# A hybrid FoX / HGRN2 / S5 layer on one core: the S5 chunk input with its four lags stacked on the contraction rows, and its weights relaid through DRAM

## What is computed

```python
x = x + 0.5 * swiglu(rms_norm(x, ffn1_norm[l]), ...)
p = rms_norm(x, mix_norm[l]) @ w_in[l]        # split into FoX q,k,v,f; HGRN2 q,f,i,g; S5 u
o_a = fox_attention(q, k, v, a_f + fox_f_bias[l])
o_b = hgrn2(b_q, b_f, b_i, lb) ... * silu(b_g)
o_c = s5_block(c_u, ...)
x = x + concat(o_a, o_b, o_c) @ w_out[l]
x = x + 0.5 * swiglu(rms_norm(x, ffn2_norm[l]), ...)
```

```python
bu = einsum('blgh,gph->blgp', u, bbar)         # real and imaginary part
x_t = lbar * x_{t-1} + bu_t                    # complex, per group and state
y_t = Re(C x_t) + D u_t ; z = gelu(y) ; out = z * sigmoid(z @ glu_w + glu_b)
```

## Time and profile before

| | us |
|---|---|
| median of three runs | 1020.2 (1020.04 to 1020.46) |
| time of the profiled execution | 1020.22 |
| span of the profiled execution | 1018.4 |
| PE busy in it | 1008.6 (99%) |
| DVE busy | 735.3 (72%) |
| ACT busy | 558.9 (55%) |
| POOL busy | 225.7 (22%) |

### The profile page before, as it was taken

The page is one execution under the profiler, slowest core; times in us unless marked ns, Lnnn a source line. Parts: engine busy times, 40 slices in busy tenths (PEclk is TensorE's granted clock), DMA queues, the critical chain, the costliest instruction groups (busy, mean ns, idle before and its releaser), DMA issues.

```text
span 1018.4 us, 20402 instructions
## 1 busy us (share of the span) xinstructions
PE 1008.6 (99%) x8434; PEld 941.2 (92%) x8434; DVE 735.3 (72%) x936; ACT 558.9 (55%) x699; POOL 225.7 (22%) x293
## 2 busy tenths in 40 slices
PE   9999999999999999999999999999999999999998
PEld 8998989999899999999999898999999998989898
DVE  7677787889878666565667867777988767565654
ACT  5646444556587645454476554456466865444441
POOL 0005999600002000000020079994000020000000
PEclk9999999999999999999999999999999999999999
DMA  8745554434325464545455454544442255454541
GB/s 305 271 161 179 192 200 170 167 125 167 111 99 207 166 218 153 213 157 213 182 199 210 158 213 166 205 166 164 138 155 90 107 221 190 184 203 167 199 172 42
DMA packets 26817, 178.38 MB, mean 175 GB/s; under 512 B 3120, under 2 KB 4160, under 8 KB 5760
## 3 DMA queue, kind: packets, MB, share of 16 engines
q1 hardware_dynamic: 25632, 173.03, 46.5%
q10 hardware_dynamic: 1008, 4.05, 1.1%
q0 software_dynamic: 112, 0.40, 0.1%
HBM read 176.42 MB, written 1.05 MB: 174 GB/s over the span
## 4 chain that ended last, share of the span: by engine, by line
PE 89%; DVE 8%; ACT 1%; DMA 1%; issue 1%; SPq 0%; DVEq 0%; ACTq 0%
PE ps L897 24%; PE ps L845 16%; PE ps L846 16%; PE ps L847 16%; PE ps L899 12%; DVE in_lo L1467 1%; DVE lo L1251 1%; DMA raw<-stream 1%; ACT hi L599 1%; PE ps L1007 1%; DVE fqk L1658 1%; PE ps L1056 0%; DVE sc L1674 0%; PE ps L1078 0%; DVE queries L1532 0%
## 5 line engine op out<-in xcount | busy, mean ns | idle before, releaser
L897 PE MATMUL ps<-xg,hi 128*128 128x512 f32 x1120 | 397.8, 399 | 0.3
L1251 DVE TENSOR_TENSOR lo<-raw,hi 128x2048 fp32r<-128x2048 f32 x130 | 303.3, 2359 | 130.8 <-ACT hi L599 130.8
L899 PE MATMUL ps<-xg,lo 128*128 128x256 f32 x1120 | 314.5, 281 | 0.0
L599 ACT ACTIVATE hi<-raw 128x2048 fp32r<-128x2048 f32 x130 | 244.7, 1911 | 108.7 <-PE ps L899 81.8
L897 PEld LDWEIGHTS ps<-xg,hi 128*128 128x128 f32 x1120 | 210.6, 188 | 52.0 <-DVE lo L1251 0.9
L899 PEld LDWEIGHTS ps<-xg,lo 128*128 128x128 f32 x1120 | 211.7, 189 | 0.0
L845 PE MATMUL ps<-act_hi,hi 128*128 128x256 f32 x704 | 199.4, 283 | 0.6 <-DVE act_lo L1304 0.6
L846 PE MATMUL ps<-act_lo,hi 128*128 128x256 f32 x704 | 199.2, 283 | 0.0
L847 PE MATMUL ps<-act_hi,lo 128*128 128x256 f32 x704 | 199.1, 283 | 0.0
L845 PEld LDWEIGHTS ps<-act_hi,hi 128*128 128x128 f32 x704 | 134.8, 191 | 2.9 <-DVE lo L1251 0.8
L847 PEld LDWEIGHTS ps<-act_hi,lo 128*128 128x128 f32 x704 | 135.0, 192 | 0.0
(11 more groups left out here) (325 smaller groups left out, 1695.0 us busy)
## 6 DMA issues: line engine op xcount, KB each, us to landing
raw<-stream SPq DMA_DIRECT2D x160, 1024.0 KB, 4.9
par<-params ACTq DMA_DIRECT2D x2, 1463.0 KB, 8.5
raw<-stream SPq DMA_DIRECT2D x8, 256.0 KB, 7.2
rows<-stream SPq DMA_DIRECT2D x2, 1024.0 KB, 7.0
x<-xT ACTq DMA_DIRECT2D x4, 256.0 KB, 6.8
out<-x SPq DMA_DIRECT2D x8, 128.0 KB, 2.0
con<-consts POOLq DMA_DIRECT2D x1, 373.5 KB, 6.2
mask<-masks POOLq DMA_DIRECT2D x1, 20.0 KB, 7.0
```

Of the source, the lines that this page charges most:

```text
L599: e.activation(hi[slot][:, :], raw[slot][:, :], ACT.Copy).then_inc(hi_written, 1)
L897: pe.matmul(bank(b), hi[slot][:, w:w + P], xg[:, k, :, :].rearrange("p s t -> p (s t)"), start=k == 0, stop=False, skip_group_check=True)
L899: last = pe.matmul(bank(b)[:, 0:T], lo[slot][:, w:w + P], xg_hi[:, k, :], start=False, stop=k == KT - 1, skip_group_check=True)
L1251: v.tensor_tensor(lo[slot][:, :], raw[slot][:, :], hi[slot][:, :].bitcast(F32), ALU.subtract).then_inc(lo_written, 1)
```

## The change

New buffers `ws` (the stacked weights: 128 rows = 4 lags x 32 channels, for both parts and eight state tiles) and `us` (the stacked u) are laid over buffers that are free at that time (`ws` over `fqk`, `us` over `fsq`). POOL writes `w_lag` to a DRAM scratch, and SP reads it back into the rows of `ws`, with the fourth lag read directly from the parameters. ACT and DVE copy u into `us`, half each. `s5_input` becomes 16 products of 128 rows, and it is called two k tiles later. The clear of `fqk` moves behind `bu_done`.

```diff
+        with ExitStack() as early:
+            ws = sb("ws", [P, 2, S5_TILES, P], F32, early)
+            sb("over_fv", [P, 2, 256], F32, early)
+            us = sb("us", [P, S5_TILES, NC], F32, early)
...
+        lag_rows = nc.dram_tensor("lag_rows", (LAG - 1, 2, P, 2 * P), F32, kind="Internal").ap()
+
+        def stack_inputs(op, q):
+
+            for i in range(LAG):
+                last = op(us[32 * i:32 * i + 32, 2 * q:2 * q + 2, :], u[32 * q:32 * q + 32, :, i * NC:(i + 1) * NC])
+            return last
...
# SP
                 for w in range(IN_UNITS):
+                    if w == RING:
+                        sp.wait_ge(units_done, l * SPLIT_UNITS + FFN_UNITS + RING)
+                        sp.wait_ge(lags_stored, l * 16 + 16)
+                        for lag in range(LAG - 1):
+                            sp.dma_start(ws[32 * lag:32 * lag + 32, :, :, :].rearrange("c a (q h) n -> c a q (h n)", h=2),
+                                         lag_rows[lag].rearrange("a (q c) n -> c a q n", c=32)).then_inc(ws_loaded, 16)
+                        for part, name in enumerate(("b_re", "b_im")):
+                            at, size = COLS[name]
+                            sp.dma_start(ws[32 * LAG - 32:, part, :, :].rearrange("c (q h) n -> c q (h n)", h=2),
+                                         params[l][:, at:at + size].rearrange("(q c) n -> c q n", c=32)
+                                         ).then_inc(ws_loaded, 16)
...
# POOL
                 steps.close()
+                pool.wait_ge(tables_ready, l * 2 + 2)
+                pool.dma_start(lag_rows.rearrange("i a r n -> r i a n"), w_lag[:, :, :, :]).then_inc(lags_stored, 16)
 
                 sum_squares(l * 3 + 1)
+                pool.memset(attn[:, :, :], 0.0).then_inc(attn_cleared, 1)
+                pool.wait_ge(bu_done, l + 1)
                 pool.memset(fqk[0:64, :, 1:FOX_HEADS:2, :], 0.0).then_inc(heads_cleared, 1)
-                pool.memset(attn[:, :, :], 0.0).then_inc(attn_cleared, 1)
...
# ACT, between split_in of unit 2 and of unit 3
                 split_in(4)
+                e.wait_ge(proj_dve, l * 9 + 1)
+                for q in (0, 1):
+                    stack_inputs(lambda dst, src: e.activation(dst, src, ACT.Copy), q).then_inc(us_act, 1)
                 split_in(4)
...
# PE
                 def s5_input():
 
-                    pe.wait_ge(proj_dve, l * 9 + 1)
-                    pe.wait_ge(tables_ready, l * 2 + 2)
-                    for i in range(LAG):
-                        for part, name in enumerate(("b_re", "b_im")):
-                            for h in range(2):
-                                for q in range(4):
-                                    r = slice(32 * q, 32 * q + 32)
-                                    w = (prm(name, h * P, P) if i == LAG - 1 else
-                                         w_lag[:, i, part, h * P:(h + 1) * P])
-                                    at = h * 256 + part * NC
-                                    last = pe.matmul(bank(q)[:, at:at + NC], w[r, :],
-                                                     u[r, h, i * NC:(i + 1) * NC],
-                                                     start=i == 0 and part == 0 and h == 0, stop=i == LAG - 1,
-                                                     skip_group_check=True)
+                    pe.wait_ge(ws_loaded, (l + 1) * (LAG + 1) * 16)
+                    pe.wait_ge(us_act, l * 2 + 2)
+                    pe.wait_ge(us_dve, l * 2 + 2)
+                    for jj in range(S5_TILES):
+                        for part in range(2):
+                            at = jj % 2 * 256 + part * NC
+                            last = pe.matmul(bank(jj // 2)[:, at:at + NC], ws[:, part, jj, :], us[:, jj, :],
+                                             start=True, stop=True, skip_group_check=True)
                     last.then_inc(bu_done, 1)
...
-                project(2, {0: s5_input})
+                project(2, {2: s5_input})
...
# DVE, behind take_lags
                 take_lags()
+                v.wait_ge(proj_dve, l * 9 + 1)
+                for q in (2, 3):
+                    stack_inputs(v.tensor_copy, q).then_inc(us_dve, 1)
                 split_in(4)
```

More of the change, by code:

```diff
@@ L319, in build @@
         bu_done = sem("bu_done")
+        lags_stored = sem("lags_stored")
+        ws_loaded = sem("ws_loaded")
+        us_act = sem("us_act")
+        us_dve = sem("us_dve")
         bu_read = sem("bu_read")
```

## The result

| | before | after |
|---|---|---|
| median, us (9 runs each) | 1019.97 | 1022.83 (1022.53 to 1023.12) |
| span of the profiled execution | 1018.4 | 1020.9 |
| ratio after to before, 95% interval | | 1.0027 (1.0019 to 1.0036) |

A forecast was written before the change was run, and what follows sets the result against it. PE, busy 99% of the span, was taken to bound the kernel. Being 1.70 us late at gate_sums in each layer, 2 x 1.70 = 3.4 us on 1020.2 gave 1023.6 us; own range 1022.3 to 1025.9, stated range 1021.0 to 1027.0.

The forecast's parts named there:

- 16 full products: PE's s5_input block: 32 records paced by weight loads 0.11 us apart, 3.52 us for 3.82, a gain of 0.30 a layer.
- DVE's copies: Eight copies on DVE ahead of unit 2's splits, 8 x 0.23 = 1.84 us; PE waits 0.55 us at project(2).
- ACT's copies: Eight copies on ACT once unit 2 is split, about 2.5 us, to 213.85; PE does not wait for them.
- bu_done: End of PE's s5_input block at 217.83, where it was 216.12; DVE's scan starts 1.71 us later.
- POOL's clear: The clear of fqk, moved behind the block's end, runs beside DVE's scan and costs it 0.25 us.
- gate_sums: PE waits 1.4 us for ACT's copy ahead of these products and is then 1.70 us late a layer; chance 0.62.
- The sum: Whole kernel: 2 x 1.70 = 3.4 us added to 1020.2, giving 1023.6 us.
- its own +1.8: Sum for the kernel with load spacing kept at 0.11 and the other two terms at their low end: +1.8 us.
- It stays: Behind gate_sums, later chains are released by PE and move with it, so the 1.70 us a layer is not absorbed.
- Transfers: POOL's store and SP's loads of ws and unit 3 cost nothing, with 3 us of cover at the slow end.
- The rival of late loads: Relaid weights or unit 3 come late in SP's queue, adding 3 us a layer: 1029.6; chance 0.12.
- The rival on the other side: Faster: full products paced by their 64 columns, not loads; block 1 to 1.9 us, time about 1016.5; chance 0.06.

The follow-up runs named there:

- e1: The kernel before with only s5_input (its 64 old products) called ahead of tile 2 of project(2), not tile 0: 1022.48 us, ratio 1.0023.
- e3: The changed kernel with gate_sums called ahead of tile 5 of project(4), not tile 2: 1020.28 us, ratio 1.0003.
- e4: The changed kernel with ACT's copy for gate_sums ahead of the four splits of unit 5, not behind them: 1020.28 us, ratio 1.0002.
- e9: The changed kernel with 32 moving columns for 64 in each of the 16 products: 1023.37 us, ratio 1.003.
- e10: The changed kernel with 64 weight columns for 128 in each of the 16 products: 1021.53 us, ratio 1.0015.
- e8: The kernel before with one lag of four in s5_input, 16 products of 32 rows for 64: 1017.54 us, ratio 0.9977.
- e5: The changed kernel with DVE's eight copies behind the first quarter of unit 2's splits, not ahead of it: 1021.77 us, ratio 1.0019.
- e6: The changed kernel with DVE's copies behind the first quarter of unit 2's splits and gate_sums ahead of tile 5 of project(4): 1019.03 us, ratio 0.9992.
- e11: The kernel before with lag_matrix done twice in layer 0 (16 products, 32 records more): 1021.16 us, ratio 1.0014.
- e2: The kernel before with s5_input ahead of tile 2 of project(2) and gate_sums ahead of tile 5 of project(4): 1021.09 us, ratio 1.0011.
- e7: The kernel before with gate_sums alone moved ahead of tile 5 of project(4), as a control: 1019.96 us, ratio 1.0001.

## Why the prediction was right

The forecast was 1023.6 by one mechanism, `gate_sums` waiting behind a later scan. The measured time is 1022.8, and the mechanism is shown by the wait in both layers, by its making in e1 and by its unmaking in e3 and e4. The sizes are less right than the mechanism: two errors cancel in it, and a term is missing. Step by step:

- *16 full products.* Estimated 3.52 us from the load spacing, measured 3.49. e9 and e10 show the reason. The Trainium skill's rule ("TensorE: Matmul & The Clock Gate", LDWEIGHTS), that a load's time goes by its columns, is borne out in kind by e10, where half the columns take 2.01 us for 3.49 (by the rule, an estimate, 32 x 64/1.2 ns = 1.71); that the rows do not matter, no run shows by itself. The estimate of 3.41 would have served as well.
- *DVE's copies.* Estimated 8 x 0.23 = 1.84, measured 1.87. The first split comes a little later behind them than I had it, and `project(2)` starts at an aligned 213.05 for my 212.85. PE is 0.75 us late there (0.59 of it shown as idle) for an estimated 0.55.
- *ACT's copies.* Estimated 2.5, measured 2.55, and hidden, as stated.
- *bu_done.* Estimated 217.83, measured 217.47, aligned 218.05. The scan is 2.02 us late for 1.71.
- *POOL's clear.* **Mis-sized**: 0.25 us estimated, nothing measured. From the scan's start to take(2) it is 9.63 us before (216.28 to 225.91) and 9.63 after (217.72 to 227.35), with the clear beside it at 217.72. I had taken the price from splits that run beside the end of the sums of squares and two clears, and put it all on the clears. The changed kernel has one clear fewer there, and its four splits (at 201.75 in DVE's timeline above) take the same 2.98 us, so the clears are not what made them long.
- *gate_sums.* Estimated 1.70 us late a layer, measured 1.76; PE's wait there is 1.09 us for an estimated 1.4. The two mis-sizings, 0.3 more on the scan and 0.25 less on the clear, cancel, so that this number fits so well is luck.
- *The sum.* 2 x 1.76 = 3.5, and 2.86 were measured. **The missing term** is PE's pause in layer 1, 0.55 us (3.93 - 3.38 in `s5_output`), which stood in the trace of before and which I had not read: with 48 products fewer per layer it is gone. 3.5 - 0.55 = 2.95, within 0.1 of the medians' difference. The lower bound of the forecast's own range, 1022.3, has no working in the prediction; its own +1.8 would give 1022.0.
- *It stays.* Right: no wait behind `gate_sums` absorbed anything.
- *Transfers.* Right that they cost nothing; the cover was 7.0 us for `ws` (206.94 to 213.98) and 4.1 us for unit 3, more than my 3 at slow rates. The rival of late loads did not occur; how late they would have to be was not tried.

The rival on the other side was priced too high in gain. I gave 1016.5 if the block took 1 to 1.9 us. The nearest run is e10, the changed kernel with a block of 2.01 us: 1021.5. e8 has a block of 1.05 us, without even the copies' wait, and is at 1017.5. My working took PE's saving as the kernel's and forgot that the scan can't begin before DVE's splits of unit 3 are done, which the copies ahead of them push back further, the same chain read from its other end.

The parts of the loss, as the runs have them: the wait for ACT's copy +2.55 us (after to e3 or e4), the wait for DVE's first split +1.1 to 1.25 (after to e5, e3 to e6), and e6's rest of -0.9. They add up to 2.8 or 2.9, but that is no check, since they are steps of one way from the changed kernel to the one before. Of the rest of -0.9, e6's trace shows the pause (0.55) and 0.02 a layer of the full products' saving, which ACT's copies hold back there; about 0.3 is not located.

## What to carry to other kernels

When a piece of work is moved on a busy engine, ask what starts when it ends. Here the engine lost nothing by the move and the time rose by 2.5 us, because a second engine's long operation hung on its end, and the way from there back to the busy engine had 0.25 us to spare; that slack can be read from two timelines before anything is built. Count products by what they take side by side and not by their number: 64 products of a quarter of the rows, four at a time, cost 3.8 us, and 16 full ones 3.5. And look for the other end of a tight chain before a saving is priced: a block that was 2.7 us shorter gave 0.9 us a layer.

## What the runs showed of the hardware that I had not expected

PE's pause for instructions is tied to a place in its stream: adding 32 records ahead of it moved it by exactly 32 (e11), and in e1, e2 and e7 it stands within one record of its old place. It is 0.29 us before, 0.35 in e1, 0.34 in e7, 1.07 in e2 and 1.09 in e11, and each time PE goes on 2.40 to 2.49 us behind the start of a 16 KB transfer on the instruction queue. So its length goes with two things: when PE comes to the place (e11) and when that transfer starts (e2). It was seen where records follow each other every 0.03 us.

e9, with 32 moving columns behind full weight loads, had a lower granted clock in layer 1 of the profiled execution. The block there is longer than layer 0's:

```profile
718.59 4.31 PE L1036 MATMUL ps<-us,ws 128*128 128x32 f32 x32
```

By stretches (us, busy time of each engine, granted clock, DMA share, GB/s):

```profile
719.00:722.00 3.00, 3.00 (x26) 3.00 (x26) 2.74 (x5) 1.61 (x4) 0.00 (x0) 0.90 0.60 180
722.00:725.00 3.00, 3.00 (x16) 3.00 (x16) 2.05 (x3) 0.00 (x0) 0.94 (x1) 0.50 1.01 401
725.00:728.00 3.00, 3.00 (x16) 3.00 (x16) 2.93 (x4) 0.63 (x1) 0.00 (x0) 0.50 0.30 126
728.00:731.00 3.00, 3.00 (x26) 3.00 (x26) 2.97 (x3) 1.85 (x3) 0.00 (x0) 0.97 0.00 0
```

The clock was 1.0 (2.4 GHz) up to about 721.4 (the first row's mean of 0.90 is 0.6 us at half), so it fell inside the block, 2.8 us behind its start, and was 0.50 (1.2 GHz) for over 6 us, with PE shown as busy throughout; ahead of the fall there were the wait of 0.59 us, two tiles of `project(2)` and most of the block. The same stretch in layer 0 kept its clock, and no other profiled execution here shows such a fall. PE's records fell to 16 in 3 us from 26, and `gate_sums` is 1.8 us later in this layer, counted from u, than in layer 0. This execution is the slowest of e9's six (1024.46; the others have 1022.69 to 1023.39, with mean granted clocks of 0.997 to 1.0), so such falls are a likely part of why e9's median is 0.5 us above the changed kernel's, but not a shown one. A block can look busy by its records and still lose the clock; why one layer and not the other stays open.
